# Feed-forward tiles in five parts of 5, 5, 4, 4, 4 instead of four of 6, 6, 5, 5, on one core

## The reference, cut to what matters

```
h  = rmsnorm(x, g)                                  # over 1024 channels
ff = silu(h @ w_gate) * (h @ w_up)                  # 1024 -> 2816 = 22 tiles of 128
x  = x + scale * (ff @ w_down)                      # 2816 -> 1024, scale 1 or 0.5
```

## Time and profile before

| | |
|---|---|
| median of 3 runs | 3575.89 us |
| profiled execution | 3575.58 us |
| its span | 3573.8 us |
| TensorE (PE) busy | 3481.6 us, 97% |
| DVE / ACT / POOL busy | 1467.3 / 963.1 / 1134.1 us |
| DMA, mean | 61 GB/s |
| matmuls | 20076 |

### The profile page before, as it was taken

One profiled execution on the slowest core, in us unless ns is written; L12 is line 12 of the kernel. 1 busy time (PEld: TensorE's weight loads), 2 busy tenths in 40 slices (PEclk: granted clock), 3 DMA queues, 4 the chain that ended last, 5 costly groups with the idle time before them and its releaser, 6 DMA issues.

```text
span 3573.8 us, 52859 instructions
## 1 busy us (share of the span) xinstructions
PE 3481.6 (97%) x20076; PEld 2931.2 (82%) x20076; DVE 1467.3 (41%) x2552; ACT 963.1 (27%) x1684; POOL 1134.1 (32%) x1499
## 2 busy tenths in 40 slices
PE   7999889999999999999999999999999999999998
PEld 5788778888888889899999878897777888888886
DVE  7966545211121263322122472837876521111214
ACT  5354433211111142111111333215663321111112
POOL 3433045322222353222222442310015532222323
PEclk9999899999999999999999999999999999999999
DMA  3112022111111121111111222111024211111113
GB/s 122 43 43 79 14 94 84 53 53 44 51 46 54 43 83 52 48 47 41 53 42 51 92 101 78 41 33 38 31 91 148 95 64 49 52 43 53 47 45 102
DMA packets 82740, 218.31 MB, mean 61 GB/s; under 512 B 20112, under 2 KB 20240, under 8 KB 82064
## 3 DMA queue, kind: packets, MB, share of 16 engines
q1 hardware_dynamic: 61936, 173.09, 15.4%
q10 hardware_dynamic: 20640, 42.95, 3.4%
HBM read 195.48 MB, written 19.46 MB: 60 GB/s over the span
## 4 chain that ended last, share of the span: by engine, by line
issue 60%; POOL 24%; PE 9%; DVE 4%; ACT 1%; POOLq 1%; DMA 0%; DVEq 0%; ACTq 0%; SPq 0%
POOL w_lo L582 24%; PE acc L744 2%; PE acc L745 2%; PE acc L746 2%; DVE cv_acc L1762 2%; PE acc L1294 0%; PE acc L1289 0%; POOLq L586 0%; PE acc L1411 0%; DVE ssq L693 0%; PE acc L1353 0%; PE acc L1420 0%; DVE cvo L1853 0%; PE acc L1428 0%; DVE tmp L705 0%
## 5 line engine op out<-in xcount | busy, mean ns | idle before, releaser
L582 POOL TENSOR_TENSOR w_lo<-w_raw,w_hi 128x256 fp32r<-128x256 f32 (+3 forms) x1480 | 1113.3, 783 | 2317.1 <-ACT w_hi L552 2316.9
L744 PE MATMUL acc<-h_hi,w_hi 128*128 128x512 f32 (+1 forms) x3520 | 1291.8, 367 | 16.5 <-issue 5.1
L745 PE MATMUL acc<-h_lo,w_hi 128*128 128x512 f32 (+1 forms) x3520 | 1283.9, 365 | 0.0
L746 PE MATMUL acc<-h_hi,w_lo 128*128 128x512 f32 (+1 forms) x3520 | 1283.2, 365 | 0.0
L744 PEld LDWEIGHTS acc<-h_hi,w_hi 128*128 128x128 f32 x3520 | 662.7, 188 | 127.6 <-issue 14.1
L745 PEld LDWEIGHTS acc<-h_lo,w_hi 128*128 128x128 f32 x3520 | 662.7, 188 | 106.0 <-issue 1.9
L746 PEld LDWEIGHTS acc<-h_hi,w_lo 128*128 128x128 f32 x3520 | 662.4, 188 | 106.1
L552 ACT CAST w_hi<-w_raw 128x1024 fp32r<-128x1024 f32 (+3 forms) x370 | 345.9, 935 | 1185.5 <-PE acc L746 1172.1
L1025 DVE TENSOR_TENSOR ff_hi<-tmp,acc 128x512 f32 (+3 forms) x154 | 94.5, 614 | 1070.5 <-PE acc L746 1039.1
L744 PE MATMUL acc<-ff_hi,w_hi 128*128 128x512 f32 (+1 forms) x1232 | 447.2, 363 | 6.4 <-POOL w_lo L582 3.2
L745 PE MATMUL acc<-ff_lo,w_hi 128*128 128x512 f32 (+1 forms) x1232 | 443.3, 360 | 0.0
(11 more groups left out here) (376 smaller groups left out, 3015.0 us busy)
## 6 DMA issues: line engine op xcount, KB each, us to landing
w_raw<-in_ffn_w_dram SPq DMA_DIRECT2D x94, 512.0 KB, 3.3
w_raw<-in_w_in_dram SPq DMA_DIRECT2D x60, 512.0 KB, 3.3
w_raw<-in_w_out_dram SPq DMA_DIRECT2D x32, 512.0 KB, 3.3
w_raw<-in_ffn_w_dram SPq DMA_DIRECT2D x48, 320.0 KB, 2.9
w_raw<-in_w_gate_dram SPq DMA_DIRECT2D x24, 512.0 KB, 3.3
w_raw<-in_w_up_dram SPq DMA_DIRECT2D x24, 512.0 KB, 3.3
w_raw<-in_ffn_w_dram SPq DMA_DIRECT2D x32, 384.0 KB, 3.0
gates_kept<-gstage ACTq DMA_DIRECT2D x32, 256.0 KB, 2.0
```

The lines of the kernel that those rows point to most:

```text
L582: pool.tensor_tensor(w_lo[:, j, a:a + step], w_raw[:, j, a:a + step], w_hi[:, j, a:a + step].bitcast(F32), ALU.subtract).then_inc(split_do ...
L744: pe.matmul(bank, wh, rh, start=(k == 0), stop=False)
L745: pe.matmul(bank, wh, rl, start=False, stop=False)
L746: ins = pe.matmul(bank, wl, rh, start=False, stop=(k == seg.kt - 1))
```

## The change

`FQ` becomes five parts. The sum stays 22.

```diff
-FQ = [6, 6, 5, 5]
+FQ = [5, 5, 4, 4, 4]
 FMAX = max(FQ)
 assert sum(FQ) == FT
```

## The result

The changed kernel takes 3595.76 us, the median of four runs (3593.22 to 3595.93); the kernel before takes 3574.61 us beside it (3572.43 to 3576.55, four runs). The ratio is 1.0058, with a 95% interval of 1.0044 to 1.0073: slower by 21 us. 3595.2 was forecast. (A fourth run of the kernel before, added to the three of the opening, moves its median from 3575.89 to 3574.61 us.)

What follows compares the result with a forecast made beforehand. The prediction took TensorE to bound the kernel, working 3481.6 of 3573.8 us. Terms 0.4 + 4.7 + 3.9 + 2.4 + 7.9 = 19.3 us took the profiled 3575.58 to 3594.9, median 3595.2 us, range 3585 to 3606.

Steps and rivals of the forecast that it cites:

- More segments: Down segments: 8 more, thinner slabs per stage, with their loads, casts, POOL pieces and additions, cost nothing.
- Handing over: Start of down segments: the first slab's second chunk waits for DVE's last split; 0.4 us in all, ends 0 and 2.
- Half a: First half of each turn: thinner slabs barely cover their chain; 0.8 us lost in turn 1, 0 in 2, 0.4 in 3.
- Half b, turns 1 and 2: Second half of these turns: DVE's and ACT's work keeps b from shortening fully; whole turns lose 4.7 and 3.9 us.
- Half b, turn 3: Third turn's second half: b becomes 26.0 us, between 24.0 and 27.9; the turn loses 2.4 us (0.5 to 4.4).
- Beside part 0: ffn1's first part: TensorE waits for the norm's last additions, then stalls with less cover; +7.9 us, ends 5.5 and 11.
- The sum: Whole kernel: the terms 0.4, 4.7, 3.9, 2.4 and 7.9 add to 19.3 us slower.
- The weight chain takes over half a: Rival, half a of the turns: cast, split and load need 3.2 us a slab, not 2.8; 3604 us, chance 0.12.
- The turns keep up: Rival, half b: DVE's pieces fill gaps, each b shortens by its 5.44 us; 3585 us, chance 0.13.
- Nothing to be seen: Rival: also part 0's additions end sooner or the stall behind them shrinks as much; 3576 to 3583 us, chance 0.07.
- Faster, by the port: Rival, half b: thinner POOL pieces free DVE until TensorE sets b; turns gain 11.7 us, 3568 us, chance 0.03.

Runs made afterwards that it cites:

- e7: Changed kernel with a constant fill instead of half a's reciprocal in the three turns: 3593.37 us, against 3595.49 for the changed kernel with the buffers of before.
- e5: Changed kernel with FMAX = 6, so every buffer lies where it lay before: 3595.49 us against 3574.93 for the kernel before, ratio 1.0055.
- e11: Changed kernel again, unedited, in a second series: 3594.22 us against 3573.41 for the kernel before, ratio 1.0059.
- e1: Kernel before with parts 5, 6, 6, 5, only the first part shorter: 3582.84 us against 3573.61, ratio 1.0025.
- e6: Kernel before with parts 6, 5, 4, 4, 3, a last part 3 deep: 3607.62 us against 3574.93, ratio 1.0090.
- e4: Changed kernel with the norm's squares and additions taken eight beside each of ffn1's up pairs 0 and 1: 3590.60 us against 3573.61 for the kernel before.

## Why the prediction was right, point by point

- **More segments, nothing.** Right: 0.2267 us a matmul in every middle segment, 43.52 us for 192.
- **Handing over, 0.4.** Too much: no segment's start shows any loss. The last split starts at 1251.48, 1.52 us behind the segment's start at 1249.96, exactly as 1239.47 was behind 1237.95, and ends within chunk 0's 2.72 us, which was the reason given. With chunk 0 at 2.04 us (depth 3) the loss is there.
- **Half a.** Forecast 22.56, 23.26 and 22.2 us; measured 22.70, 23.33 and 22.37. The chain of 2.67 us in a slab of 2.72 was close; gaps of 0.1 to 0.25 us stand at every second slab.
- **Half b, turns 1 and 2.** Forecast 31.0 and 31.5; measured 30.25 and 32.32. Losses 4.1 and 4.8 us for 4.7 and 3.9. The mechanism, DVE's work that the matmuls no longer hide, was right, but its anchor was not: it was said that 24.0 us from the reciprocal on are fixed. They are 23.0 now (1279.91 to 1302.91), and e7 shows that less than half of the reciprocal is on the path. What is nearly fixed is DVE's run from the third slab's residual on, 18.87 us. In the second turn the part from the reciprocal on grew, from 24.48 us (2029.43 to 2053.91) to 25.14 (2047.27 to 2072.41): DVE stood 1.15 us for TensorE behind the late load and the low clock, and neither was in the sum. Where the clock did not fall (e5) the turn took 54.68 us, for 54.8 forecast. The two errors have opposite signs: together the two turns lost 8.9 us for 8.6, which is partly luck.
- **Half b, turn 3.** The middle of 24.0 and 27.9 was taken, 26.0; measured 26.17. The middle was a choice, not a derivation, so its exactness shows little. The turn took 48.54 us and so lost 2.8 for 2.4; what follows it took 0.2 us less than before (16.10 for 16.34), which makes the 2.5 of the ledger.
- **Beside part 0.** Wait 5.69 for 6.4; sum to resume 21.50 for 21.4; loss above matmuls 14.6 for 14.5; against before, 8.0 for 7.9. The second stall was 3.49 us where about 2.5 were foretold. The clock did fall a second time, where I gave it half a chance (it did in all three traces of the changed kernel, after, e5 and e11, and did not in e1): 19 matmuls after the second stall took 3.62 us, about 1.3 more than at 0.121, where 0.8 was added. The short wait and the lower clock offset each other.
- **The sum** of 19.3 us has 19.4 against it in these places. The medians differ by 21.2, 20.6 and 20.8 us in three series; the 1.5 us over is 0.04% of the time, spread over stretches that are alike in both kernels, and stays without a cause. The forecast time is only 0.6 us off, but it was built on a median of the kernel before of 3575.89 us, which four runs put at 3574.61. The difference between the kernels is what was forecast, 19.3, and it is 21.

The rivals. *The weight chain takes over half a*: no; half a stayed within 0.2 us of the forecast, and where it is bound, at depth 3 (e6), ACT never stands for a load. *The turns keep up*: no; DVE's idle time lies before the third slab's residual, and 3.9 of its 5.7 us are still there. *Nothing to be seen*: no. *Faster, by the port*: its mechanism is there. DVE's run from the residual after the reciprocal to its last low part took 19.90 us before and takes 18.87 now, with the same operations; the splits that overlap POOL fell from 1.02 us to 0.95, the others stayed at 0.68:

```profile
1287.98 0.95 DVE L925 TENSOR_TENSOR h_lo<-ahead,h_hi 128x512 fp32r<-128x512 f32 x1
...
1292.65 0.68 DVE L925 TENSOR_TENSOR h_lo<-ahead,h_hi 128x512 fp32r<-128x512 f32 x1
```

That is 1.0 us of the 5 that it needed; 0.6 was the estimate. POOL's pieces are 128 wide now and take 0.43 us, and a split beside them is 0.27 longer than alone. The Trainium skill (SBUF — State Buffer, "Who interferes with whom") has the two exclude each other for a whole instruction, which agrees in kind: a shorter piece costs DVE less, yet less than a whole piece each time.

## What to carry to other kernels

When a segment hides work that does not depend on its size (a norm, an epilogue), count that work on its own engine before making the segment smaller: below its length most of the matmul time that is taken out and put elsewhere is added to the whole (here 21.2 of the last 33.0 us). Find the first operation from which the bound engine never stands, since what comes after it is worth most: taking 3 us from there gave near 3 a turn, while the reciprocal ahead of it, the longest operation of all, gave back 2.1 us of the 8.6 that were taken out in three turns. And where short work must be fitted in beside a pipeline, put it a stage earlier and split it by what one stage covers: that gained 4.6 us where making the stages thinner lost 21.

## What the runs showed of the hardware

- After 5.69 us of standing, the four sum matmuls, which in the kernel before started 1.32 us before the next one (1434.66 to 1435.98), took 2.79 us (1423.38 to 1426.17, granted clock 0.50), and after the stall of 3.49 us that followed, TensorE ran at a granted clock of 0.60 for 3.62 us.
- Stalls of about 2 us went both ways: after 2.06 us (changed kernel) the clock was 0.63 over 4.59 us, after 2.10 (e5, the same place) and 2.23 (e1, part 0) it stayed at 1.00.
- ACT's table load (1.28 us) was made during the wait, at 1421.35, 4.14 us before the root it is for (1425.49); without the wait (e4) it comes at 1418.24, 1.29 us before the first root, and on DVE's path. The wait hid the load, but the low clock behind the wait cost the sum nearly as much: the reciprocal started 2.83 us behind the sum's start with the wait, 3.02 without.
- For a weight load of 256 KB, whose median is 2.6 us, ACT stood 2.09 us while the store of `x_kept` was under way, at a DMA share of 0.91 and 325 GB/s (2041 to 2050).
- A DVE operation cut from 512 columns to 32 still took 0.35 us, against 0.81.
